# Expert weights gathered through eight slots for two tiles, with the query weights kept in place and another order at the streams

## What is computed

```
h  = x + mix @ w_out                       # mix: 4 mLSTM heads and 8 attention heads
hn = rmsnorm(h)
qp = (hn @ w_pq) as (tokens, 8 heads, 2, 128)
s  = qp . subkeys                          # (tokens, 8, 2, 128 keys)
s1, i1 = top16(s[..., 0, :]); s2, i2 = top16(s[..., 1, :])
top, sel = top16 of the 256 sums s1 + s2   # 16 experts a head, of 16,384
g = softmax(top)
y = h + sum over the 128 experts of a token:  g * gelu(peer_u[e] . hn) * peer_v[e]
y = rmsnorm(y)
```

## Time and profile before

| | |
|---|---|
| runs | 1,288.58 us median of 3 (1,286.77 to 1,292.61) |
| profiled execution | 1,286.57 us, its span 1,284.8 us |
| busy: PE, DVE, POOL, ACT | 1,123.2, 812.7, 711.5, 458.4 us |
| gathers | 384 of 1 MB, 402.68 MB |
| all bytes read | 450.82 MB |

### The profile page before, as it was taken

The page is one execution under the profiler, slowest core; times in us unless marked ns, Lnnn a source line. Parts: engine busy times, 40 slices in busy tenths (PEclk is TensorE's granted clock), DMA queues, the critical chain, the costliest instruction groups (busy, mean ns, idle before and its releaser), DMA issues.

```text
span 1284.8 us, 12644 instructions
## 1 busy us (share of the span) xinstructions
PE 1123.2 (87%) x3320; PEld 550.7 (43%) x3320; DVE 812.7 (63%) x1910; ACT 458.4 (36%) x1354; POOL 711.5 (55%) x898
## 2 busy tenths in 40 slices
PE   6999999999998899999877878878878888888886
PEld 4655656577443455555432333333223222222222
DVE  4356413669997747888977677676555555555554
ACT  2012202222443533444443343343334444434443
POOL 1000000215766656567698666666876878887760
PEclk9999999999999999999988879888998999999999
DMA  9655412148999999999999999999999999999994
GB/s 345 156 150 225 172 66 99 66 180 362 425 424 424 424 426 421 423 403 407 419 420 426 425 426 426 426 425 425 426 425 425 426 425 426 426 427 426 426 426 196
DMA packets 70179, 459.15 MB, mean 357 GB/s; under 512 B 7428, under 2 KB 15976, under 8 KB 18160
## 3 DMA queue, kind: packets, MB, share of 16 engines
q0 software_dynamic: 55296, 402.68, 74.8%
q1 hardware_dynamic: 13984, 55.17, 12.2%
q10 hardware_dynamic: 848, 0.71, 0.2%
HBM read 450.82 MB, written 7.71 MB: 357 GB/s over the span
## 4 chain that ended last, share of the span: by engine, by line
DMA 40%; PE 39%; POOL 8%; DVE 6%; issue 4%; ACT 2%; ACTq 0%; POOLq 0%; DVEq 0%; SPq 0%
DMA arena<-in_peer_uv,arena 38%; PE ps L1254 13%; PE ps L940 9%; PE ps L946 5%; POOL arena L672 4%; PE ps L1160 3%; PE ps L1240 3%; DVE arena L1717 3%; POOL arena L671 2%; POOL arena L665 1%; ACT arena L863 1%; DMA out_new_C_p<-arena 1%; DMA arena<-in_w_pq 1%; PE ps L1218 1%; PE ps L1132 1%
## 5 line engine op out<-in xcount | busy, mean ns | idle before, releaser
L1254 PE MATMUL ps<-arena 128*128 128x512 f32 x1536 | 742.7, 625 | 140.2 <-ACT arena L863 136.9
L1717 DVE CUSTOM_DVE_ANT_0 arena<-arena 128x1024 f32<-128x1024 f32 x384 | 467.5, 1231 | 300.2 <-DMA arena<-in_peer_uv,arena 297.8
L1254 PEld LDWEIGHTS ps<-arena 128*128 128x128 f32 x1536 | 287.5, 197 | 568.4 <-issue 287.7
L672 POOL DMA_INDIRECT arena<-in_peer_uv,arena x256 | 306.4, 1197 | 53.7 <-issue 46.5
L855 ACT ACTIVATE arena<-arena 128x1 f32<-128x1 f32 x384 | 77.7, 202 | 485.8 <-DVE arena L1717 484.8
L646 POOL DMA_INDIRECT arena<-in_peer_uv,arena x128 | 150.7, 1177 | 25.3 <-issue 15.1
L863 ACT ACTIVATE arena<-arena 128x128 f32<-128x128 f32 x384 | 154.2, 402 | 18.8
L857 ACT ACTIVATE arena<-arena 128x1 f32<-128x1 f32 (+1 forms) x384 | 113.1, 294 | 27.9 <-ACT arena L855 1.9
L671 POOL TENSOR_TENSOR arena<-arena 128x1 f32<-128x1 f32 x256 | 111.2, 435 | 14.6 <-POOL arena L665 8.1
L940 PE MATMUL ps<-arena 128*128 128x384 f32 (+1 forms) x336 | 111.1, 487 | 0.0
L645 POOL TENSOR_TENSOR arena<-arena 128x1 f32<-128x1 f32 x128 | 55.1, 431 | 86.3 <-PE ps L1254 84.6
(11 more groups left out here) (234 smaller groups left out, 740.1 us busy)
## 6 DMA issues: line engine op xcount, KB each, us to landing
arena<-in_w_in SPq DMA_DIRECT2D x8, 2048.0 KB, 10.7
arena<-in_w_pq SPq DMA_DIRECT2D x6, 2048.0 KB, 9.3
arena<-in_peer_uv,arena POOLq DMA_INDIRECT x384, 27.3
arena<-in_w_out SPq DMA_DIRECT2D x4, 1024.0 KB, 6.0
arena<-in_state_C SPq DMA_DIRECT2D x1, 2064.0 KB, 7.5
out_new_C_s<-arena SPq DMA_DIRECT2D x1, 2064.0 KB, 6.6
arena<-in_cache_k SPq DMA_DIRECT2D x4, 512.0 KB, 11.1
arena<-in_cache_v SPq DMA_DIRECT2D x1, 2048.0 KB, 10.7
```

The costliest lines, as they stand in the source:

```text
L672: nc.gpsimd.indirect_dma_start(slots[HALF * g + s], None, d["peer_uv"], bass.IndirectOffsetOnAxis(ap=isl[g][:, s:s + 1], axis=0)).then_inc ...
L1254: last = mm(ps[:, BANKS + half, :], diag[:, s, :], slots[SLOTS * h + s][:, DM + 512 * half:DM + 512 * half + 512], start=first and s == 0, ...
L1717: v.tensor_tensor_reduce(slots[k][:, 0:DM], slots[k][:, 0:DM], hn[t], 1.0, 0.0, ALU.mult, ALU.add, aslot[:, s:s + 1]).then_inc(a_ok, 1)
```

## The change

Both prompt tiles' queries are made one tile at a time, 128 columns ("qs" for every tile, `queries`), in the tile ahead; all four chunks of w_pq stay in place (W2, PQ1, W0, W1) until the last queries are made, and none is loaded twice. For that the eight slots of the first tile lie elsewhere, and the second tile runs in these eight as well; only the third uses sixteen. The output weights are two whole loads (`out0`, `out1`).

At the streams: the gate is a sigmoid on ACT; the head gains are multiplied in ahead of it; the prompt's gate projections, head 1's to 3's state products and the turning of the prompt's heads go behind other work; only the first two heads' queries are made ahead of the entries (`head_queries`, `head_match`, 2 x 16 products), each head with its own scores. DVE routes head 0, adds state 3, routes head 1, then begins the entries. The other heads' queries and scores are steps between pieces. Pool holds two buffers for the weighted values.

```diff
 PARTS = [(2, 0, 1, 0), (2, 1, 1, 1), (2, 2, 2, 2), (2, 4, 2, 4), (2, 6, 2, 6),
-         (0, 4, 2, 0), (0, 6, 2, 2), (0, 2, 2, 4), (0, 0, 2, 6), (1, 4, 4, 0), (1, 0, 4, 4)]
+         (0, 0, 2, 0), (0, 2, 2, 2), (0, 4, 2, 4), (0, 6, 2, 6), (1, 0, 2, 0), (1, 2, 2, 2), (1, 4, 2, 4), (1, 6, 2, 6)]
...
-        slot_after = ["qs0"] * 2 + ["qs1"] * 2 + ["hmT1"] * 4
+        slot_after = ["CN32"] + ["mo1"] * 5 + ["hmT1"] * 2
...
                         if first and not odd:
                             filled(pool, slot_after[HALF * g + s])
+                            if HALF * g + s:
+                                pool.wait_ge(state_out, 32)
...
-            sp.wait_ge(state_out, 32)
-            load_w(wbuf["PQB"], d["w_pq"][3], "pq3")
-            filled(sp, "qs3")
+            filled(sp, f"y{ORDER[2]}0")
+            load_w(wbuf["W0"], d["w_pq"][2], "pq2")
+            filled(sp, f"y{ORDER[2]}1")
+            load_w(wbuf["W1"], d["w_pq"][3], "pq3")
             sp.dma_start(gfin, d["g_fin"].partition_broadcast(P)).then_inc(gfin_in, 16)
-            filled(sp, f"y{ORDER[2]}1")
-            load_w(wbuf["W0"], d["w_pq"][1], "again1")
-            filled(sp, "qq11")
-            load_w(wbuf["PQA"], d["w_pq"][0], "again0")
...
                     if part == 0:
                         link(nc.gpsimd.memset(pad[:, 0:1], 0.0))
                         gather(n, t, 0, 0, True)
                         gather(n, t, 1, 1, True)
-                    elif n == 0:
+                    elif n < 2:
...
# query_steps: PE and ACT, piece by piece, of the first tile and of the second
+    first[1] += [("hmT", a), ("hmT", b)]
+    parts(first, 1, 1, "qs", 2, 1)
...
+    parts(first, 32, 1, "qs", 2, 3)
+    first[37] += [("sc", 2, 3)]
+    first[38] += [("hnT", a, 0), ("hnT", a, 1)]
+    for c, q in enumerate((39, 43, 47, 51)):
+        parts(first, q, 1, "qs", a, c)
+        first[q + 4] += [("sc", a, c)]
+    second[0] += [("hnT", b, 0), ("hnT", b, 1)]
+    for c, q in enumerate((1, 9, 17, 25)):
+        parts(second, q, 2, "qs", b, c)
+        second[q + 8] += [("sc", b, c)]
...
# routing_steps: DVE
+    put(0, ("gated",))
+    put(6, *sub(2, 1), *pairs(2, 2, 3), *experts(2))
...
+    put(38, *sub(2, 3), *pairs(2, 6, 7), *experts(4))
+    for t, part in ((a, 5), (b, 9)):
+        for c in range(4):
+            q = (44, 50, 56, 62)[c] if t == a else PIECES + (10, 18, 26, 34)[c]
+            put(q, *sub(t, c), *pairs(t, 2 * c, 2 * c + 1), *experts(part + c))
...
             project("mo", 2)
             head_scores(3)
             head_keys(3)
-            new_state(1)
...
             head_sum(3)
-            project("mo", 0)
+            new_state(1)
             turn_heads(2)
-            new_state(2)
...
             for i in range(2):
                 project_out("y", 2, i)
-            project("mo", 1)
+            new_state(2)
...
+            was_read(pe, "hnT21")
+            head_queries(0)
+            head_match(0)
             new_state(3)
-            was_read(pe, "hnT21")
-            stream_queries(0)
-            turn_heads(0)
-            turn_heads(1)
-            pe.wait_ge(subk_in, 16)
-            scores(2, 0)
-            stream_queries(1)
-            scores(2, 1)
-            stream_queries(2)
-            stream_queries(3)
+            head_queries(1)
+            head_match(1)
+            project("mo", 0)
+            project("mo", 1)
...
             dve.wait_ge(vals_out, 16)
-            for e in range(2):
-                route_subkeys(2, 0, (e,))
-                route_pairs(2, e, 1)
-                route_experts(e, 0)
-                route_experts(e, 1)
+            route_subkeys(2, 0, (0,))
+            route_pairs(2, 0, 1)
+            route_experts(0, 0)
+            route_experts(0, 1)
+            new_state(3)
+            route_subkeys(2, 0, (1,))
+            route_pairs(2, 1, 1)
+            route_experts(1, 0)
+            route_experts(1, 1)
```

More of the change, by code:

```diff
@@ L48 @@
 WROUNDS = HK // WIDE
-LATE = 12
 PIECE = 2
@@ L118, in psum_plan @@
     add("A", "mo2")
[L119 to L130, removed]
+    add("V", "ST3", "mkt3", "ya20", "ya21", "NUM3", *heads("CN", 3, 1))
+    add("A", "hmT2")
+    add("V", "y20", "y21", *heads("CN", 3, 2))
+    add("A", "hnT20", "hnT21", "qh0")
+    add("V", "sh0", *heads("CN", 3, 3))
+    add("A", "qh1")
+    add("V", "sh1")
+    add("A", "mo0", "mo1")
+    for what, *k in sum(query_steps()[0] + query_steps()[1], []):
+        if what in ("sc", "hnT", "hmT") or k[-1] == 0:
             add("V" if what in ("sc", "y") else "A", psum_name(what, k))
@@ L656, in gather_wide @@
                     back = WIDE
-                    if first and n == 1:
+                    if first:
                         back = SLOTS if g < 2 else 0
@@ L802, in out_gate @@
             def out_gate(t):
-                read(f"mo{t}", mo[:, t, :], ACT.Exp, bank(f"mo{t}"), scale=-1.0)
+                read(f"mo{t}", mo[t], ACT.Sigmoid, bank(f"mo{t}"))
             was_read(act, "cols")
@@ L1210, in turn_hn, with head_queries @@
                 end(last)
[L1212 to L1216 removed]
+            def head_queries(e):
+                pe.wait_ge(w_in["pq0"], 16)
+                b = begin(f"qh{e}")
+                for g in range(2):
                     for k in range(KC):
[L1218 removed]
+                        lo = P * (2 * e + g)
+                        last = mm(b[:, P * g:P * g + P], wbuf["W2"][:, k, lo:lo + P], hnT[:, k, :],
@@ L1219, in stream_queries, with head_match, queries @@
                                   start=k == 0, stop=k == KC - 1)
                 end(last)
+            def head_match(e):
+                pe.wait_ge(subk_in, 16)
+                was_read(pe, f"qh{e}")
+                b = begin(f"sh{e}")
+                for c in range(2):
+                    last = mm(b[:, P * c:P * c + P], qsT[:, 2 * e + c, :], subk[:, 2 * e + c, :], start=True, stop=True)
+                end(last)
+            def queries(t, c, part):
+                w = wbuf[query_chunk[c]]
+                if part == 0:
+                    pe.wait_ge(w_in[f"pq{c}"], 16)
+                    begin(f"qs{t}{c}")
+                b = bank(f"qs{t}{c}")
+                for k in range(KC):
+                    last = mm(b[:, P * part:P * part + P], w[:, k, P * part:P * part + P], hnT[:, k, :],
+                              start=k == 0, stop=k == KC - 1, skip_group_check=True)
+                if part == 3:
+                    end(last)
@@ L1229, in scores @@
                 end(last)
-            def prompt_query(i, part):
-                where, which = prompt_chunk[i // 4]
-                w = wbuf[where]
-                if part == 0:
-                    pe.wait_ge(w_in[which], 16)
-                    begin(f"qq{i}")
-                b = bank(f"qq{i}")
-                g = i % 4
-                for k in range(4 * part, 4 * part + 4):
-                    last = mm(b[:, 0:PROMPT], w[:, k, P * g:P * g + P], hnTP[:, k, :], start=k == 0, stop=k == KC - 1,
-                              skip_group_check=True)
-                if part == 1:
-                    end(last)
```

362 lines of the change are left out of this document (168 added, 194 removed).

## The result

The changed kernel takes 1,307.0 us (median of 4 runs, 1,304.48 to 1,307.73) against 1,287.95 (4 runs): a ratio of 1.0141, 95% interval 1.0121 to 1.0161. It is slower by 1.4%; I had forecast 1,291, with 1,299 as the upper end. The profiled execution has a span of 1,304.8 us, 20.0 more than before.

A forecast was written before the change was run, and what follows sets the result against it. Gathers through the DMA engines were taken as the bound, 946 of 1,284.8 us; -4.7 + 1.2 + 1.5 + 4.8 = +2.8 us gave 1,289.4, forecast as 1,291 after 2.0 us for the median. Own range 1,283 to 1,295; 8 in 10, 1,280 to 1,299.

The forecast's parts named there:

- Gain at the start: 4.7 us: Streams to first entries: entry 6 lands at 316.5 us, not 321.2, so 4.7 us gained, between 2 and 8.
- 5.7 us sooner: Streams' output product on PE: starts at 253.2 us, not 258.87, without tile 0's gate projection ahead of it.
- nothing else is in the DMA queues then: State's write at the start: argument against a late write, as two weight loads were in flight before.
- Entries 6 and 7: Start of the gathers: both wait for the prompt's turned heads; issue at 308 us, entry 6 landing at 316.5.
- With a landing of 8.6 us: First gathers behind the second gather's issue at 292.4 us: entry 1 lands at 301.0, entry 5 at 310.8.
- short refills: Rival, chance 0.19: gathers into idle queues may land in as little as 4.9 us; 8.0 us faster, 1,281.
- Bytes: DMA traffic behind the start: query chunk loads equal, final gains (0.5 MB) move behind entry 6; 1.2 us lost.
- First tile: Routed pieces 38 to 63: PE and DVE fall behind the DMA; 4.6 us lost, 1.5 more than before.
- The hand-over: First to second tile, in eight slots: a DMA gap of 5.6 us, 4.8 more than before, ends 0 and 8.
- At the 425.5 GB/s: Undisturbed gather rate: one entry takes 2.464 us, all 384 entries 946 us.
- if the second tile's rate stays under 420: Sign of being wrong: the second tile was expected to run at 425 GB/s behind the hand-over.
- the start does not move: Rival, chance 0.08: state's write lands with or after the old second gather, start's gain gone; +7.5 us, 1,296.

The follow-up runs named there:

- e2: Changed kernel with Pool waiting for DVE's gating product before it works out head 3's state weights; 1,299.82 us.
- e11: Changed kernel with 6 and 2 extra PE products, results overwritten, in PE's waits for the gating product and the hidden vector; 1,299.14 us.
- e7: Changed kernel with head 3's state products and sums ahead of the streams' queries, the state's write issued before routing, slots in another order; 1,294.17 us.
- e4: The kernel before the change, own layout and order, with its second tile in eight slots; 1,289.03 us, ratio 1.0013.
- e6: Changed kernel with the second tile's last routing at piece 72, not 62, and the third tile's query steps ten pieces later; 1,301.46 us.
- e5: Neither kernel: gathers alone, 16 stretches of 24 random-row gathers with slots at different addresses; 422 to 428 GB/s.
- e9: Changed kernel with 15 of 16 slots moved to 128 bytes past a multiple of 256, final gains loaded later; 1,293.06 us.

## Why the prediction was wrong

- **The start** is the step that failed: "Gain at the start: 4.7 us" was a loss. I had the second gather 5.3 us earlier than before, at 292.4; it is 10.6 later, at 308.27, past my own sign of being wrong ("after 296"). Of these 15.9 us, 5.9 are the clock ahead of the projection, most of which varies from one execution to the next. 3.1 are Pool's state weights (e2): I had DVE's gating product end at 251.9 and counted the move of head 1's state products at PE only, but there they release Pool right beside that product. 4.1 are PE's clock (e11): I took "5.7 us sooner" and 3.7 us for the products at the full clock, after taking from PE the very work that filled its waits. 2.3 are the write, which landed 10.8 us after its issue (296.78 to 307.60) where I took 8.49: "nothing else is in the DMA queues then" overlooked the first gather, issued 1.4 us ahead of it, which is likely the reason, since in e7, where no gather is ahead of it, the write takes 8.2. Together these are 15.4 of the 15.9. At entry 6, by which I reckoned the gain, the start is 8.1 us late: it lands at 329.3, and landed at 321.2 before.
- **Entries 6 and 7** waited for the turned heads, as forecast (5.78 us), and went out at 321.95 and not 308. That is 13.7 us behind the second gather where I had 15.6, so their lateness is the start's.
- **"With a landing of 8.6 us"**: the second gather, which met idle queues, landed in 5.5; the short refills' row was 4.9 and their estimate 4.4. That rival was near in this, and still the time did not fall.
- **Bytes**: I had 1.2 us more. From the second gather on 2.0 MB less were moved, worth 4.7 us; I had left out what the queues still held there before.
- **First tile**: 2.0 us lost behind the refill, to my 4.6, and less than before (4.3, where I had 3.1). Wrong in sign, small.
- **The hand-over**: 6.9 us to my 5.6. The size was about right, the cause half wrong: eight slots alone lose 2.5 there (e4), and 4.9 go when the routing behind the hand-over moves away (e6), of which 2.6 come back elsewhere.
- **"At the 425.5 GB/s"** was a term I never put in doubt. At 421 to 422 the gathers' 402.68 MB take 8 to 9 us more, though the uneven end of before hides 4 of them. The slots' addresses are the cause: gathers alone show it (e5), and with 15 slots moved the rate is 427 (e9). How six slots of sixteen gave 426 before stays open. My test "if the second tile's rate stays under 420" was set too low to see it.
- Of the rivals, "the start does not move" had the place right and the write named. It gave 1,296, for it took nothing worse than no gain.

The account: 5.9 us ahead of the projection, 4.7 from there to the second gather, 10.0 more lost in the stream and 8.0 for the rate, less 4.7 for the 2.0 MB and 4.0 for the stream's more even end. That is 19.9 of the 20.0.

## What to carry to other kernels

Work that is taken out of an engine's waits was doing something there if it kept the clock up: price the products behind the new gap at both clocks. When an instruction moves, follow everything it releases, on Pool too, and see which DVE operations then run beside it. And a new table of addresses is a change of its own: read the DMA rate of an undisturbed stretch per slot before trusting it, and see how evenly the last bytes end, since a mean over all DMA engines is not the pace of the landings.

## What the runs showed of the hardware that was not expected

- A gather's rate depends on the byte at which its slot begins: 427 to 428 GB/s at offsets of 128 and 384 bytes from a multiple of 512, 422 to 423 at 0, 16, 48, 64, 192, 256, 320 and 448. Bases of 69,632 and 139,264 change nothing at the offsets tried there (0 and 128, and 448 at the second).
- DVE products of 0.56 and 0.69 us took 2.07 and 2.28 beside Pool's, and 0.56 and 0.69 once Pool waited.
- PE at work without a gap, on products of 256 and 32 columns in turn, may fall to the half clock for 12 us and more (all of 146 to 158 in e11) in one execution and not there in another whose PE instructions and addresses up to there are the same (e6). What decides it stays open.
